# Gate products of the next head one step earlier, and a changed table of background tiles, in a two-branch encoder trunk

## The chip, the cores and the metric

The kernel runs on one core of a Trainium2 chip. The metric is the time of one execution on the device, in microseconds, as the median of several runs. The core has TensorE (PE, matrix products and transpositions, which write to PSUM), VectorE (DVE), ScalarE (ACT), GpSimd (POOL) and SyncE (SP, which issues the loads). They run side by side and wait for each other through semaphores. PSUM has eight banks of 512 float32 columns.

## The reference

Two layers are applied to 768 tokens (a request of 512 and one of 256), width 1024, and a final norm closes. One input projection feeds two branches: a bidirectional gated linear attention with 4 heads and a grouped-query attention with 16 query heads in 4 groups.

```
h = rmsnorm(x, norm_g)
proj = h @ w_in
qa, ka, va, gfl, gbl, za, qb, kb, vb, zb, ma, mb = jnp.split(proj, split_points(), axis=-1)
gf = log_sigmoid(gfl @ w_gate_f + b_gate_f) / 16       # decay of the linear heads; gb likewise
ya = gla_branch(qa, ka, va, gfl, gbl, za, ...)          # o_i = sum_j (q_i exp(b_i - b_j)) . k_j v_j, b = cumsum(g)
yb = attn_branch(qb, kb, vb, zb, ...)                   # softmax(q k) v with normed, rotated q and k
merged = jax.nn.sigmoid(ma) * ya + jax.nn.sigmoid(mb) * yb
return x + merged @ w_out
```

## The kernel before

Products of weights and activations are made in three passes with operands split in a high and a low part: ScalarE copies the loaded weights to their high part (`split`, L992), GpSimd subtracts it to get the low part (L1460), TensorE multiplies (L635 to L637). Weights come in blocks of 128 rows by 256 columns through a ring of four slots; a split is made three blocks ahead of use.

**Background.** Much of the input projection is done in the background of the latency-bound stages. A tile is 128 tokens by 256 columns of one block, three matmuls of 256 columns. Six tiles use one block, and 48 tiles fill three banks with a finished sum of 256 columns, which ScalarE copies to `stg` (L1007) and stores to DRAM. `background(start, stop)` on TensorE issues tiles, and waits for a bank (`bg_free`) where a new sum begins. How many tiles stand in which step is written in tables by hand.

**Linear heads.** The decay is applied over spans of tokens that double, in ten steps for each head, n = 0 to 9. In a step TensorE multiplies keys and queries (`L784`, later L771 and L766), then does its background tiles (`GLA_DONE`, 11 for most steps). VectorE collects the product (L1740 to L1747, in the steps of this case COPY_PREDICATED L1742), scales keys (L1726) and queries (L1728) and multiplies the decays (L1732); ScalarE merges the keys (L1109), for which the next product waits. Steps 0 to 4 finish a sum of 48 tiles, so step 5 starts with ScalarE's `store` (its copies L1007) and TensorE's first tile of step 5 waits for the first of these. Between the steps, the gates of the next head are made, in an order set by `GATE_STEP`:

- TensorE: `gla_gates` (four products, L751) behind the tiles of step GATE_STEP;
- ScalarE: `gate_magnitudes` (two, L1079) behind the merge of step GATE_STEP + 1, `gate_exps` (L1086) behind that of step + 2, `gate_logs` (L1092, with a table load) at the end of step + 3, `gate_decays` (L1098, with a table load) at the end of step + 6;
- VectorE: `gate_minimum` (L1697) at the end of steps GATE_STEP + 1 and + 2; the first waits for both magnitudes; `gate_sum` (L1705) at the end of steps + 4 and + 5.

This is done in heads 0 to 2 (a loop); head 3 has no next head. Then follow the rotation of queries and keys, attention, and the output products.

**Attention.** Each of 4 groups has 20 steps, n = 0 to 19 (4 heads by 5 units of tokens). In step n TensorE transposes the probabilities of n (`turn_p`, L838), makes the scores of n + 2 (L827, L828), in the steps of `Q_PARTS` (3, 6 and 8 in groups 1 to 3) turns a part of the queries (`turn_queries`, L813), in some steps does the value products of step n - 1 (`values`, L852, L853), and then its background tiles. ScalarE in step n makes the exponential of n + 1 (L1188), copies the transposed probabilities (`copy_pt`, L1198), the high part of turned queries (L1178), the low half of an output (`copy_low`, L1206), and last the weight splits that fall due. VectorE makes the maximum (L1868), the low part of the probabilities (L1874) and of the turned queries (L1859); `turn_p` of the next step waits for the last of these. In steps 2, 5 and others `copy_pt` also waits for the value products.

`ATT_TILES` holds the number of tiles of each step, group 0 first, then one row that is used for groups 1 to 3. From it `ATT_DONE` (tiles done after each step) is summed, and from that `start_steps` finds the step at which a block's split is due:

```
def start_steps(block, first, done, blocks):
    return {i: -1 if i * NT < first else next((n for n, d in enumerate(done) if i * NT < d), len(done))
            for i in range(block, block + blocks)}
```

Of the kernel before, what the change touches and what calls it, by code (L numbers as in the profile page):

```python
# [86 lines left out]
def spread(first, steps, *parts):  # L87


    done, at_step = [], 0  # L90
    for last, tiles in parts:
        n = last - at_step
        done += [first + -(-(tiles - first) * (i + 1) // n) for i in range(n)]
        at_step, first = last, tiles
    assert len(done) == steps
    return done


def start_steps(block, first, done, blocks):
# [8 lines left out]
GLA_GROUPS = 2 * GH + 1  # L108
GLA_TURN = GLA_FIRST + BG_TILES
GLA_DONE = spread(GLA_FIRST, GLA_STEPS, (1, GLA_FIRST + 4), (5, GLA_FIRST + KT * NT), (9, GLA_TURN - 6), (GLA_STEPS, GLA_TURN))  # L110
GATE_STEP = 3
ATT_FIRST, ATT_TAIL = (24, 6, 6, 6), 12
ATT_TILES = ((2, 2, 2, 7, 1, 2, 6, 2, 4, 3, 3, 6, 3, 3, 2, 2, 3, 2, 3, 2),) + 3 * (
    (4, 4, 2, 6, 2, 2, 6, 2, 6, 3, 3, 2, 4, 6, 3, 3, 6, 3, 6, 5),)
ATT_DONE = [[first + sum(tiles[:n + 1]) for n in range(GROUP * UNITS)] for first, tiles in zip(ATT_FIRST, ATT_TILES)]
ATT_PIECE = [done.index(KT * NT) for done in ATT_DONE]
for done, n in zip(ATT_DONE, ATT_PIECE):
# [211 lines left out]
def trunk(nc, x_prompt, x_sample, norm_g, w_in, w_gate_f, b_gate_f, w_gate_b, b_gate_b, gla_norm_g,  # L329
# [139 lines left out]
    with nc.Block() as block:  # L469
# [114 lines left out]
        def _(pe):  # L584
# [31 lines left out]
            def background(start, stop, bank0=BG_BANK, spare=0, ends=False, turned=0):  # L616


                for u in range(start, stop):
                    i, t = divmod(u, NT)  # L620
                    k = i % KT
                    if t == 0:
                        pe.wait_ge(s.w_lo_done, at("w_lo_done"))
                    end = t == NT - 1
                    if i == 0:
                        t = (t + turned) % NT
                    if turned and u == NT - turned:
                        pe.wait_ge(s.drained, at.peek("drained", 0))
                    if k == 0 and t % 2 == 0:
                        pe.wait_ge(s.bg_free, at.peek("bg_free", 1 - 3 * spare))  # L630
                        at.skip("bg_free", 1)
                    out = ps[:, bank0 * HALF + t * BGW:bank0 * HALF + (t + 1) * BGW]
                    tok = slice(t * P, (t + 1) * P)

                    mm(out, act_hi[:, k, tok], w_hi[:, k % RING, 0:BGW], start=(k == 0 and t % 2 == 0), stop=False, skip_group_check=True)  # L635
                    mm(out, act_hi[:, k, tok], w_lo[:, k % RING, 0:BGW], start=False, stop=False, skip_group_check=True)  # L636
                    last = mm(out, act_lo[:, k, tok], w_hi[:, k % RING, 0:BGW], start=False, stop=(k == KT - 1), skip_group_check=True)  # L637
                    if end:
                        last.then_inc(s.w_used, 1)
                    elif ends and k == KT - 1 and t % 2 == 1:  # L640
                        last.then_inc(s.bg_done, 1)
# [103 lines left out]
            def gla_gates():  # L745

                pe.wait_ge(s.gla_fix, at("gla_fix"))
                pe.wait_ge(s.o_read, at("o_read"))
                for d, start, n in ((0, 0, HALF), (0, HALF, TOK - HALF), (1, 0, TOK - HALF), (1, TOK - HALF, HALF)):
                    z = 2 * HALF + d * TOK + start  # L750
                    last = mm(ps[:, z:z + n], wg_fix[:, d, :], gl_t[:, start:start + n], start=True, stop=True)  # L751
                last.then_inc(s.gate_ready, 1)

            def gla_levels(h, done, more):
                for n in range(GLA_STEPS):
# [30 lines left out]
                    background(done[n - 1] if n else GLA_FIRST, done[n])  # L786
                    if more and n == GATE_STEP:
                        gla_gates()
# [191 lines left out]
        def _(act):  # L980
# [6 lines left out]
            def split(k, width=HALF):  # L987

                slot = (k + SKEW) % RING
                act.wait_ge(s.w_slot[slot], at(f"w_slot{slot}", 16))  # L990
                act.wait_ge(s.w_used, at("w_used"))
                A(w_hi[:, slot, 0:width], w_raw[:, slot, 0:width], ACT.Copy).then_inc(s.w_hi_done, 1)  # L992
# [81 lines left out]
            def gate_magnitudes():  # L1074

                act.wait_ge(s.gla_fix, at("gla_fix"))
                act.wait_ge(s.gate_ready, at("gate_ready"))
                for d in range(2):
                    A(view(gate, d * TOK, (1, TOK)), ps[:, 2 * HALF + d * TOK:2 * HALF + (d + 1) * TOK],  # L1079
                      ACT.Abs, bias=bg_fix[:, d:d + 1]).then_inc(s.gate_abs, 1)  # L1080

            def gate_exps():

                every = view(gate, 0, (1, 2 * TOK))
                act.wait_ge(s.gate_abs, at("gate_abs", 2))
                A(every, every, ACT.Exp, scale=-1.0).then_inc(s.act_chain, 1)  # L1086

            def gate_logs():

                every = view(gate, 0, (1, 2 * TOK))  # L1090
                act.wait_ge(s.act_chain, at("act_chain"))
                A(every, every, ACT.Ln, bias=1.0).then_inc(s.gate_log, 1)  # L1092

            def gate_decays():

                every = view(gate, 0, (1, 2 * TOK))
                act.wait_ge(s.gate_sum, at("gate_sum", 2))
                A(every, every, ACT.Exp, scale=1.0 / GATE_NORM).then_inc(s.gate_exp, 1)  # L1098
# [5 lines left out]
            def merge_k(n):  # L1104

                span = LEVELS[n]
                width = TOK if span < 256 else SEQS[0]
                act.wait_ge(s.k_scaled, at("k_scaled"))
                A(scaled[:, 4, 0:width], view(scaled, 2 * TOK, (2 * span, width // (2 * span)), (TOK + span, 2), (1, span)), ACT.Copy).then_inc(s.k_ready, 1)  # L1109
# [16 lines left out]
            def gla_levels(h, start, more):  # L1126
                for n in range(GLA_STEPS):
# [4 lines left out]
                    if 1 <= n < len(LEVELS):  # L1132
                        merge_k(n)
                    if more and n == GATE_STEP + 1:
                        act.wait_ge(s.totals, at.peek("totals", 1))
                        gate_magnitudes()
                    if more and n == GATE_STEP + 2:
                        gate_exps()
                    for i in start:
                        if start[i] == n:  # L1140
                            split(i, BGW)
                    if more and n == GATE_STEP + 3:
                        gate_logs()
                    if more and n == GATE_STEP + 6:
                        gate_decays()
# [442 lines left out]
        def _(dve):  # L1588
# [103 lines left out]
            def gate_minimum(d):  # L1692
                if d == 0:
                    dve.wait_ge(s.gla_fix, at("gla_fix"))
                    dve.wait_ge(s.gate_ready, at("gate_ready"))
                    dve.wait_ge(s.gate_abs, at("gate_abs", 2))
                V.tensor_scalar(view(gate_min, d * TOK, (1, TOK)), ps[:, 2 * HALF + d * TOK:2 * HALF + (d + 1) * TOK],  # L1697
                                bg_fix[:, d:d + 1], 0.0, ALU.add, ALU.min).then_inc(s.gate_used, 1)
# [18 lines left out]
            def doubled(li):  # L1717

                span = LEVELS[li]
                nb = (TOK if span < 128 else SEQS[0]) // (2 * span)  # L1720
                tot, of = block_totals(span)
                dve.wait_ge(s.q_ready, at("q_ready"))
                if li > 0:
                    dve.wait_ge(s.totals, at("totals"))
                keys = view(scaled, 2 * TOK, (TOK + span, 2), (2 * span, nb), (1, span))
                V.tensor_tensor(keys, keys, view(tot, of + 1, (TOK - 1, 2), (2, nb), (0, span)), ALU.mult).then_inc(s.k_scaled, 1)  # L1726
                queries = view(scaled, span, (TOK - span, 2), (2 * span, nb), (1, span))
                V.tensor_tensor(queries, queries, view(tot, of, (TOK + 1, 2), (2, nb), (0, span)), ALU.mult).then_inc(s.q_ready, 1)  # L1728
                if li < NMASK:
                    nb = TOK // (2 * span)  # L1730
                    out, of_out = block_totals(2 * span)
                    V.tensor_tensor(view(out, of_out, (TOK, 2), (1, nb)), view(tot, of, (TOK, 2), (2, nb)),  # L1732
                                    view(tot, of + 1, (TOK, 2), (2, nb)), ALU.mult).then_inc(s.totals, 1)
# [17 lines left out]
            def gla_levels(h, more):  # L1751
                first_queries(h)
                for n in range(GLA_STEPS):
                    collect(n)
                    if 1 <= n < len(LEVELS):
                        doubled(n - 1)
                    if more and GATE_STEP + 1 <= n < GATE_STEP + 3:
                        gate_minimum(n - GATE_STEP - 1)
# [300 lines left out]
```

## Time and profile before

| | us |
|---|---|
| median of three runs | 1930.85 (1930.23 to 1932.38) |
| the profiled execution | 1933.38 |
| its span, first to last instruction | 1931.0 |

| engine | busy us | share |
|---|---|---|
| TensorE, matmuls | 1882.5 | 97% |
| VectorE | 987.7 | 51% |
| ScalarE | 944.0 | 49% |
| GpSimd | 682.8 | 35% |

The granted clock of TensorE was 0.997 of its full 2.4 GHz. By stage, the linear heads of the first layer lie between about 164 and 400 us of the span, its attention between 487 and 754, the linear heads of the second layer between 1115 and 1352 and its attention between 1438 and 1705. Matmuls overlap: the record of a 256-column matmul is 0.28 us long, but the next one starts 0.12 us later. So TensorE's time is best read from one start to the next, and its idle time in brackets leaves out the first 0.2 us or so of a wait.

### The profile page before, as it was taken

The numbers are of one execution on the slowest core, as the hardware profiler recorded it, in microseconds if no ns is written. First come the engines' busy times: TensorE is split into PE (matmuls) and PEld (weight loads), VectorE is DVE, ScalarE is ACT, GpSimd is POOL, SyncE is SP. The second block draws the span as 40 slices with busy tenths as digits, with TensorE's granted clock in tenths as the row PEclk, the third lists the DMA queues.
The fourth block names the chain that finished last, engine by engine and source line by source line (L and its number), as shares of the span: only waits on it lengthen the run. The fifth ranks groups of instructions, "written<-read, shape, count | busy, mean of one in ns | idle before, by whom it ended". The sixth has DMA issues, their size and how long they took to land.

```text
span 1931.0 us, 38149 instructions
## 1 busy us (share of the span) xinstructions
PE 1882.5 (97%) x14864; PEld 1728.9 (90%) x14864; DVE 987.7 (51%) x1376; ACT 944.0 (49%) x1891; POOL 682.8 (35%) x688
## 2 busy tenths in 40 slices
PE   6999999999999999999999999999999999999997
PEld 6989999999999999888899899999999999988886
DVE  5113566669655554443241145657886655543324
ACT  4214555532776675423441245555337766763334
POOL 3433233258222122424653333222771221232244
PEclk9999999999999999999999999999999999999999
DMA  5322222522112114332432122225221121261323
GB/s 177 85 58 59 72 78 61 180 82 59 56 48 66 47 50 152 130 126 71 134 104 71 47 65 75 66 76 181 79 58 45 47 67 53 67 208 60 126 93 142
DMA packets 122988, 169.90 MB, mean 88 GB/s; under 512 B 15696, under 2 KB 89296, under 8 KB 122832
## 3 DMA queue, kind: packets, MB, share of 16 engines
q1 hardware_dynamic: 110880, 135.83, 23.7%
q10 hardware_dynamic: 11952, 31.86, 4.3%
q8 instruction: 113, 1.85, 0.4%
q14 instruction: 43, 0.35, 0.1%
HBM read 136.19 MB, written 31.46 MB: 87 GB/s over the span
## 4 chain that ended last, share of the span: by engine, by line
PE 89%; DVE 4%; ACT 3%; issue 3%; ACTq 1%; DMA 0%; POOL 0%; DVEq 0%
PE ps L635 12%; PE ps L636 12%; PE ps L637 12%; PE ps L589 11%; PE ps L591 11%; PE ps L590 11%; PE ps L799 4%; PE ps L838 3%; PE ps L719 2%; PE ps L852 2%; PE ps L853 2%; PE ps L827 2%; PE ps L784 2%; PE ps L828 2%; PE ps L766 1%
## 5 line engine op out<-in xcount | busy, mean ns | idle before, releaser
L1460 POOL TENSOR_TENSOR w_lo<-w_raw,w_hi 128x256 fp32r<-128x256 f32 (+1 forms) x560 | 581.4, 1045 | 1203.9 <-ACT w_hi L992 1202.8
L635 PE MATMUL ps<-w_hi,act_hi 128*128 128x256 f32 x2112 | 610.3, 289 | 6.5 <-ACT stg L1007 5.3
L637 PE MATMUL ps<-w_hi,act_lo 128*128 128x256 f32 x2112 | 597.2, 283 | 0.0
L636 PE MATMUL ps<-w_lo,act_hi 128*128 128x256 f32 x2112 | 597.1, 283 | 0.0
L992 ACT ACTIVATE w_hi<-w_raw 128x256 fp32r<-128x256 f32 (+1 forms) x560 | 273.5, 495 | 507.2 <-PE ps L591 284.2
L635 PEld LDWEIGHTS ps<-w_hi,act_hi 128*128 128x128 f32 x2112 | 403.8, 191 | 14.7 <-issue 9.6
L636 PEld LDWEIGHTS ps<-w_lo,act_hi 128*128 128x128 f32 x2112 | 404.4, 191 | 2.2
L637 PEld LDWEIGHTS ps<-w_hi,act_lo 128*128 128x128 f32 x2112 | 404.2, 191 | 0.0
L1868 DVE TENSOR_REDUCE st<-ps 128x1 f32<-128x512 f32 (+1 forms) x160 | 109.9, 691 | 126.6 <-PE ps L828 126.1
L589 PE MATMUL ps<-w_hi,o_hi 128*128 128x512 f32 x384 | 154.5, 402 | 1.7 <-DVE mb L1790 0.5
L591 PE MATMUL ps<-w_hi,o_lo 128*128 128x512 f32 x384 | 150.2, 391 | 0.0
L590 PE MATMUL ps<-w_lo,o_hi 128*128 128x512 f32 x384 | 149.8, 390 | 0.0
L1188 ACT ACTIVATE pr<-ps,st 128x512 f32<-128x512 f32 (+1 forms) x192 | 117.2, 612 | 12.0 <-DVE st L1868 9.7
L1874 DVE TENSOR_TENSOR pt_lo<-ps,pt_hi 128x512 fp32r<-128x512 f32 x128 | 88.2, 689 | 60.5 <-ACT pt_hi L1198 59.1
L1109 ACT ACTIVATE scaled<-scaled 128x768 f32<-128x768 f32 x64 | 53.2, 831 | 119.7 <-DVE scaled L1726 116.8
L1198 ACT ACTIVATE pt_hi<-ps 128x512 fp32r<-128x512 f32 x128 | 76.6, 599 | 65.9 <-PE ps L853 51.4
L838 PE MATMUL ps<-ident,pr 128*128 128x128 f32 x640 | 96.7, 273 | 7.8 <-DVE q_hl L1859 7.0
L1742 DVE COPY_PREDICATED amat<-mask,ps 128x768 f32<-128x768 uint8 x56 | 58.2, 1040 | 60.7 <-issue 48.3
L589 PEld LDWEIGHTS ps<-w_hi,o_hi 128*128 128x128 f32 x384 | 72.2, 188 | 19.1 <-issue 3.6
L589 PE MATMUL ps<-act_hi,w_hi 128*128 128x384 f32 x256 | 86.2, 337 | 0.5 <-DVE qk_t L1671 0.5
L591 PEld LDWEIGHTS ps<-w_hi,o_lo 128*128 128x128 f32 x384 | 72.1, 188 | 15.6
L591 PE MATMUL ps<-act_hi,w_lo 128*128 128x384 f32 x256 | 85.6, 334 | 0.0
(183 smaller groups left out, 3383.9 us busy)
## 6 DMA issues: line engine op xcount, KB each, us to landing
w_raw<-in_w_in SPq DMA_DIRECT2D x352, 128.0 KB, 2.1
proj<-stg ACTq DMA_DIRECT2D x36, 768.0 KB, 3.5
w_raw<-in_w_in SPq DMA_DIRECT2D x80, 256.0 KB, 2.7
w_raw<-in_w_out SPq DMA_DIRECT2D x64, 256.0 KB, 2.6
w_raw<-in_w_branch_a SPq DMA_DIRECT2D x32, 256.0 KB, 3.0
w_raw<-in_w_branch_b SPq DMA_DIRECT2D x32, 256.0 KB, 2.6
q<-proj SPq DMA_DIRECT2D x8, 768.0 KB, 8.8
zb<-proj SPq DMA_DIRECT2D x8, 768.0 KB, 9.5
```

What stands on the lines that cost most here:

```text
L589: mm(out, s_hi, m_hi, start=first, stop=False)
L590: mm(out, s_hi, m_lo, start=False, stop=False)
L591: return mm(out, s_lo, m_hi, start=False, stop=last)
L635: mm(out, act_hi[:, k, tok], w_hi[:, k % RING, 0:BGW], start=(k == 0 and t % 2 == 0), stop=False, skip_group_check=True)
L636: mm(out, act_hi[:, k, tok], w_lo[:, k % RING, 0:BGW], start=False, stop=False, skip_group_check=True)
L637: last = mm(out, act_lo[:, k, tok], w_hi[:, k % RING, 0:BGW], start=False, stop=(k == KT - 1), skip_group_check=True)
L838: last = nc.tensor.transpose(bank(pt_bank(n))[:, place * P:(place + 1) * P], pr[:, n % 2, j * P:(j + 1) * P], ident[:])
L992: A(w_hi[:, slot, 0:width], w_raw[:, slot, 0:width], ACT.Copy).then_inc(s.w_hi_done, 1)
L1188: last = A(pr[:, n % 2, i * w:(i + 1) * w], ps[:, n % 2 * HALF + i * w:n % 2 * HALF + (i + 1) * w], ACT.Exp, bias=nmax(n, i), accum_out=de ...
L1460: G.tensor_tensor(w_lo[:, slot, 0:width], w_raw[:, slot, 0:width], w_hi[:, slot, 0:width].bitcast(F32), ALU.subtract).then_inc(s.w_lo_done, 1)
L1868: V.tensor_reduce(out, view_ps(n % 2 * HALF, (HALF // k, k), (1, HALF // k)), AX.X, ALU.max, negate=True).then_inc(s.neg_max, 1)
L1874: V.tensor_tensor(p_turned(n, True), src, p_turned(n, False).bitcast(F32), ALU.subtract).then_inc(s.pt_lo_ready, 1)
```

## The change

The step behind which the next head's gate products stand goes from 3 to 2, and all that is placed relative to it on ScalarE and VectorE goes with it. In the tile table of attention groups 1 to 3, steps 3 and 6 get 8 tiles instead of 6, step 1 gets 2 instead of 4 and step 8 gets 4 instead of 6. The sums after step 8 are as before.

```
-GATE_STEP = 3
+GATE_STEP = 2
 ATT_FIRST, ATT_TAIL = (24, 6, 6, 6), 12
 ATT_TILES = ((2, 2, 2, 7, 1, 2, 6, 2, 4, 3, 3, 6, 3, 3, 2, 2, 3, 2, 3, 2),) + 3 * (
-    (4, 4, 2, 6, 2, 2, 6, 2, 6, 3, 3, 2, 4, 6, 3, 3, 6, 3, 6, 5),)
+    (4, 2, 2, 8, 2, 2, 8, 2, 4, 3, 3, 2, 4, 6, 3, 3, 6, 3, 6, 5),)
```

ScalarE in a linear head, from the merge of step 4 (L1109) to the copies of the finished sum in step 5 (L1007), before the change:

```order
 L1109 ACTIVATE scaled<-scaled 128x768
 L1135 ISA
 L1076 REGISTER_ALU
 L1077 REGISTER_ALU
 L1079 ACTIVATE gate<-ps,bg_fix 128x768 x2
 L991 REGISTER_ALU
 L992 ACTIVATE w_hi<-w_raw 128x256
 L1017 REGISTER_ALU
 L1018 ISA
 L1007 ACTIVATE stg<-ps 128x512 x3
```

The same place after it:

```order
 L1109 ACTIVATE scaled<-scaled 128x768
 L1085 ISA
 L1086 ACTIVATE gate<-gate 128x1536
 L991 REGISTER_ALU
 L992 ACTIVATE w_hi<-w_raw 128x256
 L1017 REGISTER_ALU
 L1018 ISA
 L1007 ACTIVATE stg<-ps 128x512 x3
```

Between merge and copies the exponential stands in place of the two magnitudes; the magnitudes now stand behind the merge of step 3, ahead of that step's two splits.

VectorE in a linear head, from the key scaling of step 3 (blocks of 4) to that of step 4 (blocks of 8), after the change:

```order
 L1726 TENSOR_TENSOR scaled<-scaled,totals 128x2x96x4
 L1728 TENSOR_TENSOR scaled<-scaled,totals 128x2x96x4
 L1732 TENSOR_TENSOR totals<-totals 128x2x96
 L1694 REGISTER_ALU
 L1695 REGISTER_ALU
 L1696 ISA
 L1697 TENSOR_SCALAR gate_min<-ps,bg_fix 128x768
 L1736 REGISTER_ALU
 L1742 COPY_PREDICATED amat<-mask,ps 128x768
 L1722 REGISTER_ALU
 L1724 REGISTER_ALU
 L1726 TENSOR_TENSOR scaled<-scaled,totals 128x2x48x8
```

The first minimum (L1697) now stands ahead of the collect of step 4 (L1742); before, it stood ahead of that of step 5.

ScalarE in attention group 1, steps 1 and 2; the first row shown is the exponential for step 2, and the rows with a sign are the piece of the difference:

```order
 L1188 ACTIVATE pr,st<-ps,st 128x512
 L1198 ACTIVATE pt_hi<-ps 128x4x128
-L992 ACTIVATE w_hi<-w_raw 128x256
-L1188 ACTIVATE pr,st<-ps,st 128x512
-L1198 ACTIVATE pt_hi<-ps 128x4x128
-L1206 ACTIVATE o_low<-ps 64x256
+L1188 ACTIVATE pr,st<-ps,st 128x512
+L1198 ACTIVATE pt_hi<-ps 128x4x128
+L1206 ACTIVATE o_low<-ps 64x256
+L992 ACTIVATE w_hi<-w_raw 128x256
 L1188 ACTIVATE pr,st<-ps,st 128x256 x2
 L1198 ACTIVATE pt_hi<-ps 128x4x128
```

The split of block 2 went from behind step 1's copy to behind step 2's low output, ahead of the exponential for step 4. GpSimd's and SP's orders are the same in both kernels.

## Rows read from the trace of the kernel before

**Rows 1.** The page's busy table: busy us, share of the span, instructions.
```profile
PE 1882.5 (97%) x14864; PEld 1728.9 (90%) x14864; DVE 987.7 (51%) x1376; ACT 944.0 (49%) x1891; POOL 682.8 (35%) x688
```

**Rows 2.** TensorE's waits, whole span: waited for, us in total, times, longest.
```profile
PE ps L838 <- DVE q_hl L1859: 7.0, 14, 0.6
PE ps L635 <- ACT stg L1007: 5.3, 11, 0.7
```

**Rows 3.** Timeline of TensorE, head 0: start, us, instruction, [idle before <- releaser].
```profile
198.28 0.87 PE L751 MATMUL ps<-gl_t,wg_fix 128*128 128x512 f32 x4
199.08 0.63 PE L784 MATMUL ps<-scaled 128*32 128x32 f32 x48
...
203.78 0.63 PE L784 MATMUL ps<-scaled 128*32 128x32 f32 x48
205.10 0.35 PE L635 MATMUL ps<-w_hi,act_hi 128*128 128x256 f32 x1 [0.69 <-ACT stg L1007]
```

**Rows 4.** Timeline of ScalarE in the same steps, 4 and 5 of head 0.
```profile
201.74 0.84 ACT L1109 ACTIVATE scaled<-scaled 128x768 f32<-128x768 f32 x1 [3.20 <-DVE scaled L1726]
202.49 1.68 ACT L1079 ACTIVATE gate<-ps,bg_fix 128x768 f32<-128x768 f32 x2
204.06 0.41 ACT L992 ACTIVATE w_hi<-w_raw 128x256 fp32r<-128x256 f32 x1
204.36 1.57 ACT L1007 ACTIVATE stg<-ps 128x512 f32<-128x512 f32 x3
...
207.79 1.47 ACT L1086 ACTIVATE gate<-gate 128x1536 f32<-128x1536 f32 x1
209.16 0.70 ACT L992 ACTIVATE w_hi<-w_raw 128x256 fp32r<-128x256 f32 x2
```

**Rows 5.** Timeline of VectorE in the same steps.
```profile
199.84 1.03 DVE L1742 COPY_PREDICATED amat<-mask,ps 128x768 f32<-128x768 uint8 x1 [2.41 <-issue]
...
204.20 1.02 DVE L1697 TENSOR_SCALAR gate_min<-ps,bg_fix 128x768 f32<-128x768 f32 x1 [1.46 <-ACT gate L1079]
205.14 1.04 DVE L1742 COPY_PREDICATED amat<-mask,ps 128x768 f32<-128x768 uint8 x1
206.06 0.95 DVE L1726 TENSOR_TENSOR scaled<-scaled,totals 128x768 f32<-128x768 f32 x1
```

**Rows 6.** Timelines of GpSimd (head 0, step 5) and VectorE (head 1, step 2).
```profile
209.64 1.44 POOL L1460 TENSOR_TENSOR w_lo<-w_raw,w_hi 128x256 fp32r<-128x256 f32 x2 [4.36 <-ACT w_hi L992]
...
245.83 1.51 DVE L1728 TENSOR_TENSOR scaled<-scaled,totals 128x768 f32<-128x768 f32 x1
```

**Rows 7.** Timeline of TensorE in attention group 1, layer 1, steps 2 to 9.
```profile
565.48 0.28 PE L853 MATMUL ps<-pt_lo,v_hl 128*128 128x256 f32 x1
...
570.37 0.63 PE L838 MATMUL ps<-ident,pr 128*128 128x128 f32 x4 [0.55 <-DVE q_hl L1859]
...
576.55 0.28 PE L635 MATMUL ps<-w_hi,act_hi 128*128 128x256 f32 x1
576.91 0.28 PE L635 MATMUL ps<-w_hi,act_hi 128*128 128x256 f32 x1
...
578.51 0.63 PE L838 MATMUL ps<-ident,pr 128*128 128x128 f32 x4
...
585.17 0.63 PE L838 MATMUL ps<-ident,pr 128*128 128x128 f32 x4 [0.54 <-DVE q_hl L1859]
```

**Rows 8.** Timeline of ScalarE in the same group, steps 2, 3 and 5.
```profile
565.86 0.60 ACT L1198 ACTIVATE pt_hi<-ps 128x512 fp32r<-128x512 f32 x1 [1.50 <-PE ps L853]
566.48 0.38 ACT L1206 ACTIVATE o_low<-ps 64x256 f32<-64x256 f32 x1
566.89 0.48 ACT L1188 ACTIVATE pr<-ps,st 128x256 f32<-128x256 f32 x1
...
574.55 0.38 ACT L1206 ACTIVATE o_low<-ps 64x256 f32<-64x256 f32 x1 [0.16 <-PE ps L853]
...
575.27 0.69 ACT L1188 ACTIVATE pr<-ps,st 128x512 f32<-128x512 f32 x1
```

## The prediction

> **What bounds the kernel now.** I read the page's busy table first: TensorE is busy for 97% of the span [rows 1]. So only two things can move the time: work added to or taken from TensorE, and stretches in which it waits. The change keeps every matmul and only moves some, so I looked at the waits. The view of TensorE's waits has two entries that lie where the change works [rows 2]: the transposition of probabilities (L838) waits 14 times for the low part of the turned queries, 7.0 us together, and a background tile (L635) waits 11 times for ScalarE's copy of a finished sum out of PSUM (`stg` L1007), 5.3 us together. Six of those eleven are in the linear heads, at step 5; twelve of those fourteen are in attention groups 1 to 3 of both layers, at steps 3 and 8. Matmuls overlap in these records, so I work with distances between starts, which also show waits too short for that view. Steps are counted from 0.
>
> **Linear heads, where step 5 begins now.** TensorE starts step 4's product at 199.08 and step 5's at 203.78, 4.70 apart, and step 5's first tile only at 205.10, after 0.69 of idleness [rows 3]. It waits for a bank. The bank's sum was complete when step 5's product began, but ScalarE starts the copy only at 204.36 [rows 4], because the two gate magnitudes (L1079, from 202.49) and a weight split (L992, from 204.06) stand ahead of it. Copy start to first tile is 0.74. So this wait is set by ScalarE's queue ahead of L1007, and what the change puts there is the question. Times are those of head 0 of the first layer; the six repetitions (three heads, two layers) show the same distances within 0.01.
>
> **What the move of the gate products does.** TensorE's four products (198.28 to 199.08, 0.80) go from the end of step 3 to the end of step 2. Up to step 4's product it has the same work, so that stays at 199.08, and nothing is won or lost there; gates and their bank are free in step 2, since GpSimd's gate weights (L1483) are a step 1 job and the previous head's outputs have been read before step 1. Step 3's product now ends its step without gates behind it, so it starts one plain step of 4.70 earlier: 199.08 - 4.70 = 194.38. From there I copy the present distances of step 4 [rows 3 to 5]:
> - magnitudes at +3.41 (202.49 - 199.08): 197.79;
> - VectorE's first minimum (L1697, which waits for both magnitudes) at +5.12: 199.50;
> - VectorE's next collect (L1742) can start only behind it, at +6.06: 200.44. Today step 4's collect starts at 199.84. So it comes **0.60 later**.
>
> ScalarE's merge of the keys waits for that collect and the scaling behind it, and the exponential now stands right behind this merge. Collect to the work behind the merge is 202.49 - 199.84 = 2.65, so the exponential starts at 203.09. It takes 209.16 - 207.79 = 1.37 up to the next instruction, against 204.06 - 202.49 = 1.57 for the two magnitudes that it replaces: 0.20 won. Split at 204.46, and 0.30 later the copy at **204.76 instead of 204.36**. The change shortens the queue ahead of the copy by 0.20 and delays its head by 0.60: step 5's wait grows by 0.40. Step 5's product itself stays at 203.78, for the merge starts 201.74 - 199.84 = 1.90 behind the collect and takes 0.84: it ends at 203.18. 6 x 0.40 = **+2.4 us**.
>
> The rest of the move I cost at nothing. Magnitudes, logarithm (with its table load), sums and last exponential each fall one step earlier, into steps of about 4.7 us in which both engines idle now (VectorE 1.46 ahead of the minimum alone [rows 5]). The splits queued behind the magnitudes in step 3 come later by the 1.57 of these and by the delay of the step itself (under 0.8), but serve blocks of weights three blocks on, 18 tiles or some 6.5 us; if that cover were gone the price would be the excess over it. The last exponential leaves ScalarE freer before the head's second store, which is hidden under the head's value products anyway. SP's and GpSimd's queues keep their order.
>
> **What the tiles do.** A tile is three matmuls, 576.91 - 576.55 = 0.36 [rows 7]; two are 0.72. Take group 1 of the first layer. Step 1 loses two, so step 2's value products end at 565.60 - 0.72 = 564.88 (their last starts at 565.48, and one takes 0.12), and ScalarE's copy of step 2 (L1198, which waits for them) at 565.86 - 0.72 = 565.14 [rows 7, 8]. From here to step 4's first transposition runs one chain: copy, low output (L1206), next exponential, copy of step 3, high queries, low queries. It is 570.37 - 565.86 = 4.51 long and leaves TensorE idle for 0.55 at its end. But the tile table also sets when splits are due. Block 2 (tiles 12 to 17) begins after 14 done tiles at step 1 now, and after 12 it begins at step 2, so its split moves from behind step 1's copy to between L1206 and the exponential: into this chain. With a split there the distance is 575.27 - 574.55 = 0.72, without one 566.89 - 566.48 = 0.41 [rows 8]: +0.31. Step 4 begins at 570.37 - 0.72 + 0.31 = 569.96, **0.41 earlier**.
>
> Step 6 has a hidden wait: six tiles behind its second tile's start, 576.55, would end at 576.55 + 5 x 0.36 = 578.35, yet step 7 begins at 578.51. With eight tiles TensorE itself sets the end: 576.55 - 0.41 + 7 x 0.36 = 578.66, **0.15 later than today**. Step 8 is given four tiles instead of six. It too ends in a wait for the low queries (0.54 [rows 7]); the chain to step 9 hangs on step 7's value products, so it keeps its distance, 585.17 - 578.51 = 6.66, and the two tiles taken away only lengthen the wait by 0.72. Step 9 begins at 585.32 with as many tiles done as today (40). Per group: step 3's wait shrinks, step 6's goes, step 8's grows by as much and the split eats the rest, +0.15. 6 groups: **+0.9 us**.
>
> **Sum**: 2.4 + 0.9 = +3.3 us on the profiled span of 1931.0. That execution took 1933.38, the median of the three is 1930.85; I add the difference to the median: **1934.1 us**, 0.17% more.
>
> **Rivals.**
> A. *GpSimd and VectorE collide in step 4 (slower).* The delayed splits of step 3 reach GpSimd at about 199.36 + 0.48 = 199.84 (split to subtraction, 209.16 to 209.64) and two subtractions last 1.44: until 201.28 [rows 4, 6]. VectorE's key scaling (L1726) would start at 200.44 + 0.92 = 201.36. The margin is 0.08. Where GpSimd holds on, a scaling of this kind takes 1.51 instead of 0.95 [rows 5, 6]: 0.56 more ahead of the merge, hence ahead of the copy. It decides from the point where GpSimd is late by more than that margin: 6 x 0.56 = 3.4, together +6.7: 1937.5.
> The Trainium skill (SBUF - State Buffer, Who interferes with whom) says that a VectorE instruction with two SBUF inputs contends with GpSimd's reads and that whoever issues first holds the shared ports for its whole instruction. By that rule the trace agrees, and the price would be only what is left of GpSimd's instruction, between nothing and the full amount.
> B. *The minimum does not hold up the collect*, so only the shorter exponential counts: 6 x -0.20 = -1.2, with the tiles -0.3: 1930.5. Against it: today the collect of step 5 does stand behind the minimum, 204.20 then 205.14, with its product already there.
> C. *The split finds a gap*: then the whole 0.72 is kept at step 3, step 7 begins at 576.55 - 0.72 + 7 x 0.36 = 578.35 and a group gains 0.16: -1.0, with the heads +1.4: 1932.3. Against it: ScalarE has its next exponential ready to go behind L1206 today, so an instruction between them is paid in full.
> D. *B and C at once*, the change doing what its words suggest: -2.2: 1928.7.
>
> **How the numbers follow.** Forecast 0.55, A 0.15, B 0.10, C 0.12, D 0.04, anything else 0.04. A measurement of this kernel tells apart about 0.2%, 3.9 us, so slower begins at 1934.7. The forecast case spreads about 1.3 to either side (the 0.40 and the 0.15 are differences of starts good to 0.1, six times each; medians of runs move by about 1), so over a third of it, 0.20, lies above that line; with A 0.15 and 0.03 of the rest, slower is 0.38. Faster needs less than 1927.0: 0.03. Same 0.59. The range takes in the forecast, A, C and most of B: 1930.0 to 1937.8.
>
> **What would show it.** In the changed profile, heads 0 to 2: collect of step 4 right behind L1697, at 6.06 from step 3's product; L1007's first copy in step 5 at about 5.68 from step 4's product (now 5.28); TensorE's idleness before step 5's first tile 1.1 (now 0.69). If L1726 of step 4 takes over 1.0, it is A; if the idleness is 0.5, it is B. Attention: idleness before step 4 shrinks from 0.55 to about 0.1 to 0.2, none before step 7, and before step 9 about 1.25; an idleness of zero before step 4 says C. I am wrong in kind if another wait of TensorE over 0.3 appears, at step 2's gate products or at step 2's value products of attention, which find their low probabilities ready with nothing to spare.

## The result and the profile after

| | us |
|---|---|
| before, median of 20 runs | 1932.05 (1930.23 to 1934.54, and one of 4758.09) |
| changed, median of 20 runs | 1935.24 (1933.4 to 1937.48) |
| ratio changed to before | 1.0017, 95% interval 1.0010 to 1.0024 |
| span of the profiled execution, changed | 1933.6 (before 1931.0) |

The change costs 3.2 us, 0.17%. TensorE's busy time is nearly the old one (1881.3 us after 1882.5); of the waits, the two that lie where the change works grew. Its view of waits over the whole span of the changed kernel (waited for, us in total, times, longest), against [rows 2]:

```profile
PE ps L838 <- DVE q_hl L1859: 7.9, 8, 1.3
PE ps L635 <- ACT stg L1007: 7.5, 11, 1.1
```

The wait for the copy of a finished sum grew by 2.2 us (5.3 before). The wait for the turned queries has 8 entries instead of 14, and yet its sum grew by 0.9: the six ahead of step 4 fell from 0.55 to 0.13 and are no longer listed, and the six ahead of step 9 grew from 0.54 to 1.26. The span of the profiled execution grew by 2.6 us: by 2.3 in heads 0 to 2 and 0.8 in attention, less 0.2 in head 3 and 0.3 outside these stages, where nothing was changed (the last section shows how such stretches vary).

**Linear heads.** Timelines of the changed kernel, head 0 of layer 1, steps 4 and 5: TensorE, ScalarE, VectorE, GpSimd. They answer to [rows 3 to 6].

```profile
198.90 0.63 PE L784 MATMUL ps<-scaled 128*32 128x32 f32 x48
203.60 0.63 PE L784 MATMUL ps<-scaled 128*32 128x32 f32 x48
205.31 0.36 PE L635 MATMUL ps<-w_hi,act_hi 128*128 128x256 f32 x1 [1.07 <-ACT stg L1007]
```

```profile
197.61 1.67 ACT L1079 ACTIVATE gate<-ps,bg_fix 128x768 f32<-128x768 f32 x2
199.17 0.72 ACT L992 ACTIVATE w_hi<-w_raw 128x256 fp32r<-128x256 f32 x2
202.16 0.85 ACT L1109 ACTIVATE scaled<-scaled 128x768 f32<-128x768 f32 x1 [2.26 <-DVE scaled L1726]
202.91 1.47 ACT L1086 ACTIVATE gate<-gate 128x1536 f32<-128x1536 f32 x1
204.29 0.40 ACT L992 ACTIVATE w_hi<-w_raw 128x256 fp32r<-128x256 f32 x1
204.59 1.55 ACT L1007 ACTIVATE stg<-ps 128x512 f32<-128x512 f32 x3
```

```profile
199.32 1.02 DVE L1697 TENSOR_SCALAR gate_min<-ps,bg_fix 128x768 f32<-128x768 f32 x1 [1.35 <-ACT gate L1079]
200.25 1.04 DVE L1742 COPY_PREDICATED amat<-mask,ps 128x768 f32<-128x768 uint8 x1
201.17 0.95 DVE L1726 TENSOR_TENSOR scaled<-scaled,totals 128x768 f32<-128x768 f32 x1
```

```profile
199.66 1.43 POOL L1460 TENSOR_TENSOR w_lo<-w_raw,w_hi 128x256 fp32r<-128x256 f32 x2 [5.54 <-ACT w_hi L992]
```

Read them from step 4's product, 198.90. The collect L1742 starts 1.35 behind it, where it was 0.76, because the minimum L1697 stands before it and waits for the magnitudes L1079. The copy L1007 starts 5.69 behind it, where it was 5.28. GpSimd ends at 201.09 and the key scaling L1726 starts at 201.17 and lasts 0.95: the two miss each other by 0.08. Step 5's first tile comes after 1.07 of idleness. The other five repetitions show 1.06 to 1.07.

**Attention.** TensorE in group 1 of layer 1 of the changed kernel, steps 4, 6, 7 and 9, against [rows 7]:

```profile
569.92 0.63 PE L838 MATMUL ps<-ident,pr 128*128 128x128 f32 x4
...
576.09 0.28 PE L635 MATMUL ps<-w_hi,act_hi 128*128 128x256 f32 x1
...
578.61 0.60 PE L838 MATMUL ps<-ident,pr 128*128 128x128 f32 x4
...
585.24 0.63 PE L838 MATMUL ps<-ident,pr 128*128 128x128 f32 x4 [1.26 <-DVE q_hl L1859]
```

ScalarE in steps 2 and 3 there, against [rows 8]:

```profile
565.11 0.60 ACT L1198 ACTIVATE pt_hi<-ps 128x512 fp32r<-128x512 f32 x1 [1.17 <-PE ps L853]
565.73 0.38 ACT L1206 ACTIVATE o_low<-ps 64x256 f32<-64x256 f32 x1
566.01 0.41 ACT L992 ACTIVATE w_hi<-w_raw 128x256 fp32r<-128x256 f32 x1
566.44 0.47 ACT L1188 ACTIVATE pr<-ps,st 128x256 f32<-128x256 f32 x1
```

The group starts at 559.00 (559.06 before). Step 4 begins 0.45 earlier than before the change, step 7 0.10 later, step 9 0.07 later, or 0.39 earlier, 0.16 later and 0.13 later when counted from the group's start. The split now lies between L1206 and the exponential: 0.71 from one to the other, 0.41 before.

### The profile page after: what moved, and what is told of

The parts are those of the page before. It is cut to its first block, busy times and chain, and to the rows that moved or that the text cites. A ratio compares the mean times of both kernels' runs of the same rounds, so it can differ in the third digit from the quotient of the medians.

```text
span 1933.6 us, 38149 instructions
## 1 busy us (share of the span) xinstructions
PE 1881.3 (97%) x14864; PEld 1728.8 (89%) x14864; DVE 987.8 (51%) x1376; ACT 941.9 (49%) x1891; POOL 682.6 (35%) x688
## 4 chain that ended last, share of the span: by engine, by line
PE 91%; DVE 4%; ACT 2%; issue 2%; ACTq 1%; DMA 0%; POOL 0%; DVEq 0%
PE ps L635 13%; PE ps L636 12%; PE ps L637 12%; PE ps L589 11%; PE ps L591 11%; PE ps L590 11%; PE ps L799 4%; PE ps L838 3%; PE ps L719 2%; PE ps L852 2%; PE ps L853 2%; PE ps L784 2%; PE ps L827 2%; PE ps L828 2%; PE ps L766 1%
## 5 line engine op out<-in xcount | busy, mean ns | idle before, releaser
L1109 ACT ACTIVATE scaled<-scaled 128x768 f32<-128x768 f32 x64 | 53.1, 830 | 125.9 <-DVE scaled L1726 123.0
L1742 DVE COPY_PREDICATED amat<-mask,ps 128x768 f32<-128x768 uint8 x56 | 58.0, 1036 | 56.9 <-issue 44.7
```

## The experiments

All runs were timed in five rounds beside the kernel before. Where an effect is under 2 us the interval of its ratio is wider than the effect, and the distances between starts in the trace carry the verdict; they repeat in the six heads within about 0.02, and the change of a group's time differs from that of group 1 by at most 0.07. The run e7 has 7 executions, e8 has 5 and the others 11. In the table, "per repetition" is the change of the time of a linear head (first product to first product, 54.32 before for heads 1 and 2) or of an attention group (first to last transposition of probabilities, 53.67 in group 1).

| run | ratio to before (95%) | median less before, us | per repetition, us | times six |
|---|---|---|---|---|
| e1_gates_only | 1.0012 (1.0003 to 1.0022) | +2.1 | +0.37 | +2.2 |
| e2_tiles_only | 1.0005 (0.9996 to 1.0014) | +1.0 | +0.13 | +0.8 |
| e3_products_only | 1.0006 (0.9996 to 1.0015) | +1.6 | +0.01 | +0.1 |
| e4_minimum_late | 1.0004 (0.9995 to 1.0013) | +1.1 | +0.18 | +1.1 |
| e5_exp_late | 0.9989 (0.9980 to 0.9998) | -2.1 | -0.38 | -2.3 |
| e6_tiles_split_kept | 0.9995 (0.9986 to 1.0004) | -0.5 | -0.17 | -1.0 |
| e7_table | 0.9969 (0.9958 to 0.9980) | -5.7 | -1.09 | -6.5 |
| e8_both | 0.9953 (0.9939 to 0.9966) | -9.2 | -0.40 and -1.12 | -9.1 |
| e9_splits_first | 0.9997 (0.9988 to 1.0006) | -0.6 | -0.19 | -1.1 |
| e10_step8_kept | 0.9982 (0.9973 to 0.9991) | -2.9 | -0.61 | -3.7 |

### The two parts alone

The run e1 makes only the first edit of the change:

```
-GATE_STEP = 3
+GATE_STEP = 2
```

> Only the gate step goes from 3 to 2; the tile table stays as before. Theory (ScalarE's queue ahead of the copy L1007: a shorter instruction in it, but its head held back by the collect behind the first minimum): six times +0.37 to +0.40, so +2.2 to +2.4 us against before, and TensorE's idleness ahead of step 5's first tile about 1.07 in heads 0 to 2. Rival (the two parts only lose together, or the median's +3.2 is all from the tiles): 0.

TensorE's waits in this run:

```profile
PE ps L635 <- ACT stg L1007: 7.5, 11, 1.1
PE ps L838 <- DVE q_hl L1859: 7.0, 14, 0.6
```

The first row is that of the changed kernel, the second that of before. The run e2 makes only the edit of the table:

```
-    (4, 4, 2, 6, 2, 2, 6, 2, 6, 3, 3, 2, 4, 6, 3, 3, 6, 3, 6, 5),)
+    (4, 2, 2, 8, 2, 2, 8, 2, 4, 3, 3, 2, 4, 6, 3, 3, 6, 3, 6, 5),)
```

> Only the tile table is changed, the gate step stays 3. Theory (step 3's wait filled, step 6's gone, step 8's grown, the split of block 2 paid in the chain): six times +0.13 to +0.16, +0.8 to +0.9 us. Rival (tiles in turning steps fill waits as the words of the change say, and the loss is all the gates'): six times -0.3, about -2 us.

```profile
PE ps L838 <- DVE q_hl L1859: 8.0, 8, 1.3
PE ps L635 <- ACT stg L1007: 5.3, 11, 0.7
```

Here it is the other way round: the copy's wait is that of before, the wait for the queries is the changed one. The parts lie in separate stages and add: +2.2 and +0.8 make +3.0 by the traces, +2.1 and +1.0 make +3.1 by the medians, against +3.2 for both. The rival that lays all the loss on one part falls. For e2 alone the interval holds zero; its sign rests on the trace.

### Is it the place of the products, or the queue?

On the kernel before, e3 moves the products alone:

```
 background(done[n - 1] if n else GLA_FIRST, done[n])
-if more and n == GATE_STEP:
+if more and n == GATE_STEP - 1:
     gla_gates()
```

> TensorE's four gate products alone go to step 2; ScalarE's and VectorE's gate work stays where it was before (magnitudes behind the merge of step 4), tile table as before. Theory: step 4's product starts when it did and the queue ahead of L1007 is the old one, so 0 (within 0.3 us), idleness ahead of step 5's first tile 0.69. Rival (the products' own place costs, by their bank or by a later step 3): +2.2 us as in the gate step's move alone.

The idleness ahead of step 5's first tile is 0.69 to 0.70 in all six heads, and a head takes 54.33. So moving TensorE's products by themselves moves nothing. The median is 1.6 above before, but its interval reaches from 0.8 below to 2.9 above; no distance in heads 0 to 2 or in attention shows such a loss. Part of it is the clock: 6 of the 11 executions have a granted clock of 0.997, but only 9 of the 33 of the kernel before beside them, and at the same clock the mean spans differ by 0.8 us (0.997) and 0.3 us (0.998). The rest stays open.

On e1, e4 moves the two minimums one step later:

```
 GATE_STEP = 2
-if more and GATE_STEP + 1 <= n < GATE_STEP + 3:
-    gate_minimum(n - GATE_STEP - 1)
+if more and GATE_STEP + 2 <= n < GATE_STEP + 4:
+    gate_minimum(n - GATE_STEP - 2)
```

> Gate step 2 with its magnitudes and exponential, but both minimums of VectorE one step later (ends of steps 4 and 5), so that none stands between the magnitudes and step 4's collect; tile table as before. Theory: the collect of step 4 is back at 0.76 behind its product, only the shorter exponential counts: copy L1007 0.2 earlier than before the change, six times -0.2, -1.2 us, idleness 0.5. Rival (the longer wait comes from the exponential itself or from the splits behind the magnitudes): +2.2 us as with the gate step alone.

This missed. VectorE and GpSimd in step 4 of head 0 (the product starts at 199.17):

```profile
199.94 1.04 DVE L1742 COPY_PREDICATED amat<-mask,ps 128x768 f32<-128x768 uint8 x1 [1.70 <-issue]
200.87 1.32 DVE L1726 TENSOR_TENSOR scaled<-scaled,totals 128x768 f32<-128x768 f32 x1
```

```profile
199.94 1.44 POOL L1460 TENSOR_TENSOR w_lo<-w_raw,w_hi 128x256 fp32r<-128x256 f32 x2 [5.56 <-ACT w_hi L992]
```

The collect is back at 0.77 behind its product, as expected. But now the key scaling comes up at 200.87, while GpSimd is busy until 201.38, and takes 1.32 instead of 0.95. Copy at 5.49 behind the product, idleness 0.87: half the loss is gone, not all of it. This looks like the collision of rival A, which the minimum ahead of the collect had kept away in the changed kernel. If it is that, it must go when GpSimd is done earlier. On e4, e9 puts the splits of step 3 ahead of the magnitudes (two places of the kernel, what lies between them left out):

```
 merge_k(n)
-if more and n == GATE_STEP + 1:
-    act.wait_ge(s.totals, at.peek("totals", 1))
-    gate_magnitudes()
...
 for i in start:
     if start[i] == n:
         split(i, BGW)
+if more and n == GATE_STEP + 1:
+    act.wait_ge(s.totals, at.peek("totals", 1))
+    gate_magnitudes()
```

> The kernel with gate step 2 and late minimums, and in it ScalarE's two splits of step 3 ahead of the magnitudes instead of behind them; old tile table. In the run with late minimums step 4's key scaling took 1.32 us instead of 0.95 and the copy L1007 began 5.49 behind step 4's product instead of the 5.08 expected. Theory: it was held by GpSimd's second subtraction, which the late splits put there; with the splits first GpSimd is done before the collect, the scaling takes 0.95 again, the copy begins at 5.08, idleness ahead of step 5's first tile 0.49, six times -0.2, -1.2 us against before. Rival (the longer scaling has another cause, as the magnitudes' reads of PSUM or a later collect): 1.3 us again, idleness 0.87, +1.1 us.

Steps 3 and 4 of head 0, GpSimd and VectorE:

```profile
198.85 0.73 POOL L1460 TENSOR_TENSOR w_lo<-w_raw,w_hi 128x256 fp32r<-128x256 f32 x1 [0.32 <-ACT w_hi L992]
```

```profile
199.37 1.04 DVE L1742 COPY_PREDICATED amat<-mask,ps 128x768 f32<-128x768 uint8 x1 [1.70 <-issue]
200.30 0.95 DVE L1726 TENSOR_TENSOR scaled<-scaled,totals 128x768 f32<-128x768 f32 x1
```

GpSimd ends at 199.58, the scaling takes 0.95, and the idleness before step 5's first tile is 0.495 in each of the six heads: what had been expected of e4. The collect comes 0.77 behind its product, as in e4, and the magnitudes lie nearer to the scaling than there (they end at 200.36, in e4 at 199.56), so neither of these two made it longer; GpSimd's subtraction did. The gate step's price comes apart: the shorter exponential -0.19 a head (e9), the collision +0.37 (e4 less e9) or the collect behind the minimum +0.56 (e1 less e9), and of the last two only one acts at a time: a collect that is late starts the scaling behind GpSimd's end.

### What stands ahead of the copy

On e1, e5 moves the exponential one step later:

```
 GATE_STEP = 2
-if more and n == GATE_STEP + 2:
+if more and n == GATE_STEP + 3:
     gate_exps()
```

and in the same way the logarithm, the last exponential and the sums one step later.

> Products, magnitudes and minimums by gate step 2, but exponential, logarithm, sums and last exponential where they were before (steps 5, 6, 7 and 8, 9); tile table as before. Only merge and split then stand ahead of the copy L1007 in step 4. Theory: the merge ends at 203.2 in head 0's times in spite of the minimum, so the copy starts when TensorE's last tile is seen, about 204.0 instead of 204.36: idleness ahead of step 5's first tile 0.3, six times -0.4, -2.4 us. Rival (the delay of 0.60 of the collect reaches the copy whatever stands in the queue): +1 us or more.

ScalarE, head 0, step 4 into step 5, and TensorE's wait:

```profile
200.80 0.85 ACT L1109 ACTIVATE scaled<-scaled 128x768 f32<-128x768 f32 x1 [2.25 <-DVE scaled L1726]
201.56 0.40 ACT L992 ACTIVATE w_hi<-w_raw 128x256 fp32r<-128x256 f32 x1
202.45 1.58 ACT L1007 ACTIVATE stg<-ps 128x512 f32<-128x512 f32 x3 [0.49 <-PE ps L637]
```

```profile
203.19 0.36 PE L635 MATMUL ps<-w_hi,act_hi 128*128 128x256 f32 x1 [0.30 <-ACT stg L1007]
```

The merge still comes late, for the collect still stands behind the minimum, but now ScalarE is the one that waits, 0.49 for TensorE's last tile. What remains, 0.30, stands behind a copy that waits for nothing on its own engine: from its start to the tile it is 0.74, as before the change. The rival (the delay reaches the copy whatever stands in the queue) falls. This is the form in which the move of the gate products pays: -2.1 us.

### The tiles

```
+for starts in ATT_START[1:]:
+    starts[2] = 1
```

in addition to the changed table, with gate step 3.

> The changed tile table, but the split of block 2 in groups 1 to 3 stays behind step 1's copy; gate step 3. Theory: the chain to step 4 is 0.31 shorter again, step 3's whole 0.72 is kept, step 7 is bound by TensorE's own work: a group gains 0.16, -1.0 us, no idleness ahead of step 4's first transposition. Rival (the split costs nothing where it is; the loss is in the tiles): +0.8 us, as with the table alone.

Step 3 takes 4.06 again instead of 4.35, and the idleness ahead of step 4's first transposition is zero, where it was 0.14 in e2. A group takes 53.50 instead of 53.80 in e2. The split's 0.3 is what turns a gain of 0.17 a group into a loss of 0.13; the medians differ in the same direction (-0.5 and +1.0), but the interval of each holds zero.

The run e10 has the changed table, but steps 9 and 10 give the two tiles in place of step 8:

```
-    (4, 4, 2, 6, 2, 2, 6, 2, 6, 3, 3, 2, 4, ...
+    (4, 2, 2, 8, 2, 2, 8, 2, 6, 2, 2, 2, 4, ...
```

> Gate step 3; the changed table with step 8 keeping its 6 tiles, and steps 9 and 10 giving one each (2 and 2): what step 8's share costs by itself. Block 2's split stays in the chain to step 4 as in the changed table. Theory: step 9 begins where it does with the changed table (+0.14 a group) but with two tiles more done, so a group gains 0.72 - 0.14 = 0.58, -3.5 us; idleness ahead of step 9 falls from 1.26 to 0.54. Rival (the chain to step 9 moves with the tiles, or steps 9 to 11 give the gain back): +0.8 us as with the changed table alone.

```profile
PE ps L635 <- ACT stg L1007: 5.3, 11, 0.7
PE ps L838 <- DVE q_hl L1859: 3.6, 8, 0.5
```

The wait ahead of step 9 is 0.54 again and the sum of this row halves. Steps 9 and 10 each take 0.36 less with a tile less, and nothing later gives it back. So the two tiles taken from step 8 were the dearest edit of the table: 0.74 a group.

The table of e7 fills step 8's wait as well and leaves block 2's split in step 1:

```
-    (4, 4, 2, 6, 2, 2, 6, 2, 6, 3, 3, 2, 4, ...
+    (4, 3, 2, 7, 2, 2, 6, 2, 8, 2, 2, 2, 4, ...
```

> Gate step 3, another table for groups 1 to 3: steps 1, 3, 8, 9, 10 get 3, 7, 8, 2, 2 tiles instead of 4, 6, 6, 3, 3. Done after step 1 are 13, so block 2's split stays in step 1; step 8's wait is filled instead of lengthened. Theory: step 3 gains 0.36, step 8 two tiles for nothing (0.72 less what TensorE's own work exceeds, 0.02): 1.06 a group, -6.4 us, if steps 9 and 10 hold with 2 tiles. Rival (steps 9 to 11 turn into waits for the probabilities when they are short): less than half of it, -3 us or nothing.

A group takes 52.58: 1.09 less. Step 8 takes 4.06 with eight tiles, where it took 4.04 with six, and the wait before step 9 is gone. Steps 9 and 10 are one tile shorter each without a new wait. The median gains 5.7 us.

### Both together

> The late exponential (products, magnitudes and minimums by gate step 2, the rest as before) together with the other table (steps 1, 3, 8, 9, 10: 3, 7, 8, 2, 2). Theory: the two lie in separate stages and add: -2.4 - 6.4 = -8.8 us. Rival: less than the sum of the two alone by over 1 us.

```profile
PE ps L635 <- ACT stg L1007: 2.9, 11, 0.3
PE ps L784 <- issue: 2.9, 4, 1.4
PE ps L650 <- DVE act_lo L1625: 1.7, 1, 1.7
PE ps L838 <- DVE q_hl L1859: 1.5, 8, 0.2
```

1922.49 us, 0.47% less than before (ratio 0.9953, 0.9939 to 0.9966): -9.2 us, against -7.8 for the sum of its parts by the medians, within their intervals, and -9.1 against -8.8 by the traces. It beats both kernels. The two waits that the prediction began with fell from 5.3 to 2.9 and from 7.0 to 1.5.

## Why the prediction was right

The prediction said 1934.1 from a median of 1930.85, +3.3; measured +3.2 (1935.24 against 1932.05 in the longer series). The time itself is 1.1 above the forecast, because the kernel before has a median 1.2 higher in that series than in its first three runs. By the distances the change costs 3.0 to 3.1 (+0.37 to +0.38 a head and +0.10 to +0.17 a group, six of each), 0.2 to 0.3 less than the sum.

- **Step 4's product stays, step 3's starts 4.70 earlier than it.** So it was: 194.19 and 198.90, 4.71 apart.
- **Collect 0.60 later.** It came at 1.35 behind its product instead of 0.76: 0.59. The first minimum is 5.12 behind step 3's product in the sum and 199.32 - 194.19 = 5.13 in the trace.
- **Copy 0.40 later.** 5.69 against 5.68 foreseen. Wait of TensorE +0.37 to +0.38 a head, a little under 0.40. e4 and e9 show that the term is made as the sum made it, and e5 that it is the queue.
- **The rest at nothing.** e3 shows it for the products. In the changed kernel, all other steps of heads 0 to 2 have their old length within 0.02.
- **Attention.** Step 4 0.41 earlier: 0.39. Step 7 0.15 later: 0.16. Step 9 0.15 later: 0.13. e6 shows the split's 0.31 (0.29 to 0.30), e10 step 8's 0.72 (0.74).
- **Rival A**, the collision, did not happen in the changed kernel: the margin, put at 0.08, was 0.08. In e4 it did happen, with the collect on time, and the price can be read there. The scaling ends at 202.19, 0.81 behind GpSimd's last subtraction (201.38). The 1.51 of [rows 6], from which the prediction took its price, ends in the same way: at 247.34, 0.82 behind the subtraction that was running when it came up (its row stands below this list). The twelve instructions of L1728 and L1732 on 128x768 that take 1.5 us in the kernel before and the six scalings of 1.32 us in e4 all end 0.81 or 0.82 behind the GpSimd instruction that they met. So what is paid is GpSimd's rest, and neither a fraction nor a fixed price. The Trainium skill (SBUF - State Buffer, Who interferes with whom) says that the one that comes first keeps the shared ports for its whole instruction. The trace agrees, by those ends. Here the prediction was not right: it let A cost the full 0.56 as soon as GpSimd was late by more than the margin. By an estimate from these rows (an unhindered scaling takes 0.95, so it loses 0.14 less than the rest of GpSimd's instruction) A costs nothing until GpSimd is about 0.2 us later than the prediction had it, and the full 0.56 only when it is about 0.8 later. The forecast does not rest on this, only the place of A in the range.
- **Rivals B, C and D** fall: the minimum does hold up the collect, and the split is paid. B's effect took e9 to bring about (-0.19 a head), C's took e6 (-0.17 a group).

```profile
245.14 1.38 POOL L1460 TENSOR_TENSOR w_lo<-w_raw,w_hi 128x256 fp32r<-128x256 f32 x1 [0.24 <-issue]
```

What the agreement does not prove: a median moves by about a microsecond from series to series (before: 1930.85, 1932.05, 1932.15, 1931.72, 1931.99), so that +3.2 and +3.3 are this close is partly luck. The distances, which were foreseen one by one, are not.

## What to carry to other kernels

Where a wait is set by an in-order queue, list what stands between the event and the awaited instruction, and for each of these what it waits for itself: here a shorter instruction was put in the place of a longer one (-0.2), and its start was held back by three times as much (+0.6) through another engine. A table of background work that also sets when side work falls due changes two things at once; look at the order on the other engines before moving a number. Filling a wait pays only if the filler does not come from a step that ends in such a wait itself: two tiles moved from step 1 into step 3's wait brought step 4 forward by 0.68 us (e6), and two taken out of step 8, which ends in such a wait, cost 0.74 (e10).

## What the hardware showed that was not expected

Head 3 of either layer, which the change leaves alone, has waits of TensorE that nothing in the profile releases. One, of 0.57 to 0.64 us ahead of step 2's product, stands in both layers of all twelve profiles. A second differs from profile to profile, from none in e1 and 0.3 in e2, e4 and e9 to 1.43 in e8. Before, it is in layer 1, step 5, in the middle of a product:

```profile
368.44 0.27 PE L784 MATMUL ps<-scaled 128*32 128x32 f32 x8 [1.16 <-issue]
```

In the changed kernel this one is gone, and one stands in layer 2, at step 4:

```profile
1316.14 0.67 PE L784 MATMUL ps<-scaled 128*32 128x32 f32 x48 [0.73 <-issue]
```

By these, head 3 of the changed kernel is 1.0 us shorter in layer 1 and 0.8 longer in layer 2. All others that have it have it in layer 1, step 5. Which of code loading, loads of data or something else makes them was not tried, and each kernel has one profile, so whether the place goes with the kernel or with the execution is not shown.

Head 0 of layer 1 starts anywhere from 180.13 (e2) to 181.81 (e4), and here the traces show the cause: TensorE's clock between 19 and 24 us, in the first products with weights (L650, L651). The row from 19.2 to 22.8, before and in e1 (behind the engines' busy times come the granted clock, the DMA share and GB/s):

```profile
19.20:22.80 3.60, 3.52 (x13) 3.52 (x14) 0.03 (x1) 3.60 (x11) 3.56 (x3) 0.60 0.33 80
19.20:22.80 3.60, 3.58 (x20) 3.58 (x21) 0.47 (x1) 3.60 (x12) 3.52 (x3) 1.00 0.30 81
```

These products begin at 19.29 and 19.22, and then the matmuls of 384 columns follow each other every 0.32 us before and every 0.18 in e1. In e1, e2 and e5 the granted clock stays at 1.00 (2.4 GHz) there, and head 0 starts at 180.1 to 180.2; in the other nine profiles it falls for most of this stretch to 0.50, the lower level of 1.2 GHz (0.53 to 0.69 over the row), and head 0 starts at 181.3 to 181.8. Just before, TensorE waits for VectorE (L650 for `act_lo`), idle for 1.52 to 1.67 us in the three and for 1.75 to 2.36 in the nine. No edit of this case touches that place. The profiles of before and changed are both among the nine, so their comparison above is not touched by it.

Together these are as large as most effects studied here, and are why a single span says little: e1 lost 2.1 us at the median and has a shorter span than before, 1930.6, with the full clock at the start and without the second wait in head 3. The clock at the start may reach the medians too. Of the 77 executions of the kernel before beside the experiments, the 23 with a granted clock of 0.997 have a mean span of 1930.3 us, the 48 with 0.998 one of 1929.3. That this is the clock at the start is not shown, for these executions have no profile; it fits in size, since 1.6 us are 0.0008 of the span.
